# Layer norm of a two-layer decoder: order of sums, column products, mean spreads, root and first centering around the last tile

## The reference, cut to what matters

```python
def layer_norm(x, g, b):
    mu = jnp.mean(xf, axis=-1, keepdims=True)
    var = jnp.mean(jnp.square(xf - mu), axis=-1, keepdims=True)
    y = (xf - mu) * lax.rsqrt(var + LN_EPS)
    return (y * g + b)
...
for l in range(DEPTH):
    h = layer_norm(a * h + 0.5 * swiglu(h, ...), ln1_g[l], ln1_b[l])      # norms 1 and 4
    y = concat(pool_mixer(...), gla_mixer(...)) @ w_out[l]
    h = layer_norm(a * h + y, ln2_g[l], ln2_b[l])                         # norms 2 and 5
    h = layer_norm(a * h + 0.5 * swiglu(h, ...), ln3_g[l], ln3_b[l])      # norms 3 and 6
```

## Time and profile before

| | |
|---|---|
| median of 3 runs | 1818.94 us (1815.22 to 1819.45) |
| the profiled execution | 1817.18 us, its span 1815.5 us |
| PE busy | 1789.5 us, 99% of the span |
| DVE, ACT, POOL busy | 1424.3, 1164.0, 327.3 us |
| mean granted clock of TensorE | 0.99 of full speed |
| chain of work that ended last | PE 93%, DVE 4%, ACT 2% |
| column means on DVE (L1761) of norms 1 to 6 start at | 355.38, 556.59, 909.98, 1262.23, 1459.38, 1802.71 us |

### The profile page before, as it was taken

One profiled execution on the slowest core, in us unless ns is written; L12 is line 12 of the kernel. 1 busy time (PEld: TensorE's weight loads), 2 busy tenths in 40 slices (PEclk: granted clock), 3 DMA queues, 4 the chain that ended last, 5 costly groups with the idle time before them and its releaser, 6 DMA issues.

```text
span 1815.5 us, 37552 instructions
## 1 busy us (share of the span) xinstructions
PE 1789.5 (99%) x14440; PEld 1743.4 (96%) x14440; DVE 1424.3 (78%) x2545; ACT 1164.0 (64%) x2030; POOL 327.3 (18%) x366
## 2 busy tenths in 40 slices
PE   8999999999999999999999999999999999999997
PEld 8999999999999999999999999999998879999996
DVE  6988888668557988888688888886684589888886
ACT  5777676574347667676576676765743477777764
POOL 2111212211000121212301111122110111212113
PEclk9999999999999999999999999999999999999998
DMA  6675767556554676767556757565665656767662
GB/s 194 152 181 131 179 134 159 130 134 131 116 125 102 167 176 136 170 143 159 140 126 146 182 129 180 130 165 125 137 135 121 129 110 162 181 137 185 132 167 70
DMA packets 114081, 263.54 MB, mean 145 GB/s; under 512 B 10736, under 2 KB 37872, under 8 KB 113904
## 3 DMA queue, kind: packets, MB, share of 16 engines
q1 hardware_dynamic: 68112, 167.86, 31.9%
q0 software_dynamic: 45504, 92.29, 30.4%
q10 hardware_dynamic: 288, 0.98, 0.2%
HBM read 259.00 MB, written 2.10 MB: 144 GB/s over the span
## 4 chain that ended last, share of the span: by engine, by line
PE 93%; DVE 4%; ACT 2%; issue 1%; DMA 0%; ACTq 0%; SPq 0%; DVEq 0%
PE PS L629 21%; PE PS L630 21%; PE PS L631 21%; PE PS L608 4%; PE PS L609 3%; PE PS L610 3%; PE PS L563 3%; PE PS L565 3%; PE PS L564 3%; PE PS L599 2%; PE PS L573 2%; PE PS L574 2%; PE PS L927 1%; PE PS L770 1%; PE PS L758 1%
## 5 line engine op out<-in xcount | busy, mean ns | idle before, releaser
L503 POOL DMA_DIRECT2D w_lo<-in_stream x316 | 270.0, 854 | 1403.1 <-ACT w_lo L1138 1368.2
L1134 ACT ACTIVATE s_hi<-s_sum 128x512 fp32r<-128x512 f32 (+1 forms) x496 | 291.2, 588 | 153.2 <-PE PS L631 144.4
L1588 DVE TENSOR_TENSOR s_lo<-s_sum,s_hi 128x512 fp32r<-128x512 f32 (+1 forms) x496 | 293.5, 632 | 2.9 <-ACT s_hi L1134 2.7
L629 PE MATMUL PS<-v_hi,s_hi 128*128 128x264 f32 (+1 forms) x912 | 258.5, 283 | 0.0
L631 PE MATMUL PS<-v_hi,s_lo 128*128 128x264 f32 (+1 forms) x912 | 257.8, 283 | 0.0
L630 PE MATMUL PS<-v_lo,s_hi 128*128 128x264 f32 (+1 forms) x912 | 257.7, 283 | 0.0
L631 PE MATMUL PS<-x_hi,w_lo 128*128 128x264 f32 (+1 forms) x656 | 185.6, 283 | 0.0
L629 PE MATMUL PS<-x_hi,w_hi 128*128 128x264 f32 (+1 forms) x656 | 185.5, 283 | 0.0
L630 PE MATMUL PS<-x_lo,w_hi 128*128 128x264 f32 (+1 forms) x656 | 185.4, 283 | 0.0
L630 PEld LDWEIGHTS PS<-v_lo,s_hi 128*128 128x128 f32 x912 | 172.1, 189 | 0.0
L629 PEld LDWEIGHTS PS<-v_hi,s_hi 128*128 128x128 f32 x912 | 171.6, 188 | 0.0
(11 more groups left out here) (272 smaller groups left out, 5700.9 us busy)
## 6 DMA issues: line engine op xcount, KB each, us to landing
raw<-in_stream SPq DMA_DIRECT2D x164, 512.0 KB, 4.3
w_lo<-in_stream POOLq DMA_DIRECT2D x160, 256.0 KB, 4.6
spare<-in_stream SPq DMA_DIRECT2D x72, 512.0 KB, 6.5
w_lo<-in_stream POOLq DMA_DIRECT2D x60, 512.0 KB, 7.5
raw<-in_stream SPq DMA_DIRECT2D x48, 384.0 KB, 4.6
spare<-in_stream SPq DMA_DIRECT2D x48, 384.0 KB, 5.3
w_lo<-in_stream POOLq DMA_DIRECT2D x96, 192.0 KB, 4.7
X<-in_x_t SPq DMA_DIRECT2D x8, 264.0 KB, 6.7
```

What stands on the lines that cost most here:

```text
L503: pool.dma_start(w_lo[:, slot, to], stream[n // RAWS, n % RAWS, :, part], accum_op=ALU.add).then_inc(lo_added[slot], 16)
L629: nc.tensor.matmul(o, hi[:, w], r_hi, start=start and k == 0, stop=False, skip_group_check=True)
L1134: nc.scalar.activation(s_hi[:, j - 1, w], s_sum[:, j - 1, w], ACT.Copy).then_inc(S["s_hi_done"], 1)
L1588: V.tensor_tensor(s_lo[:, j - 1, w], s_sum[:, j - 1, w], s_hi[:, j - 1, w].bitcast(F32), ALU.subtract).then_inc(S["s_lo_done"], 1)
```

## The change

It touches nothing but order and waits around the end of `resid` and the beginning of `norm`, in all six norms.

- PE: M1 goes from behind Q1 to behind Q2. The order becomes C1, Q1, C2, Q2, M1, M2, R.
- DVE, sums: the square of tile 6 is added behind `add_last(0)`; `add_last(1)` stands ahead of `last_sum(0)`.
- DVE, norm: the reciprocal stands ahead of `center_first(0)`. In norms 1 to 5 tile 0 is centered straight from PSUM, as the last norm did already, so it waits for PE's spread and no longer for ACT's copy; tile 1 waits for the copy.
- ACT: the root stands ahead of the first copy of the mean. In norms 1 to 5 each copy waits until DVE has centered that half of tile 0 from the same PSUM half.

```diff
--- before.py
+++ after.py
@@ -780,12 +780,12 @@
                 columns(0, sum_x, 0)
                 pe.wait_ge(S["s2_first"], LN + 1)
                 columns(1, sum_sq, 0)
-                spread_mean(0).then_inc(S["mean_first"], 1)
 
                 pe.wait_ge(S["s1_done"], LN * 7 + 7)
                 columns(0, sum_x, 1).then_inc(S["mean_acc"], 1)
                 pe.wait_ge(S["s2_done"], LN * 7 + 7)
                 columns(1, sum_sq, 1).then_inc(S["msq_acc"], 1)
+                spread_mean(0).then_inc(S["mean_first"], 1)
                 pe.wait_ge(S["resid_done"], LN * KC + KC)
                 spread_mean(1).then_inc(S["mean_spread"], 1)
                 pe.wait_ge(S["rstd_done"], LN + 1)
@@ -1282,13 +1282,17 @@
                 def copy_mean(p):
                     return nc.scalar.activation(mean[:, tokens(span, p)], part(1, span, p), ACT.Copy)
 
-                act.wait_ge(S["mean_first"], LN + 1)
-                copy_mean(0).then_inc(S["mean_first_copied"], 1)
                 act.wait_ge(S["var_done"], LN + 1)
                 n_tok, blocks = stat_blocks(span)
                 nc.scalar.activation(col_std[0:n_tok, 0:blocks], col_var[0:n_tok, 0:blocks], ACT.Sqrt)\
                     .then_inc(S["std_done"], 1)
+                act.wait_ge(S["mean_first"], LN + 1)
+                if not final:
+                    act.wait_ge(S["centered_first"], LN + 1)
+                copy_mean(0).then_inc(S["mean_first_copied"], 1)
                 act.wait_ge(S["mean_spread"], LN + 1)
+                if not final:
+                    act.wait_ge(S["centered"], LN * KC + 1)
                 copy_mean(1).then_inc(S["mean_copied"], 1)
                 g = C_LN + 16 * r
 
@@ -1694,7 +1698,8 @@
                             dve.wait_ge(S["s1_done"], LN * 7 + (mo - 1))
                         V.tensor_tensor(sum_x[:, tok], X[:, 0, tok] if mo == 1 else sum_x[:, tok], X[:, mo, tok],
                                         ALU.add).then_inc(S["s1_done"], 1)
-                        add_square(mo)
+                        if mo < KC - 2:
+                            add_square(mo)
 
                 k = KC - 1
                 dve.wait_ge(S["s1_done"], LN * 7 + 6)
@@ -1721,8 +1726,9 @@
                         .then_inc(S["s2_done" if p else "s2_first"], 1)
 
                 add_last(0)
+                add_square(KC - 2)
+                add_last(1)
                 last_sum(0)
-                add_last(1)
                 last_square(0)
                 last_sum(1)
                 last_square(1)
@@ -1738,9 +1744,8 @@
                 def center_first(p):
 
                     h = tokens(span, p)
-                    if final:
-                        return V.tensor_tensor(X[:, 0, h], X[:, 0, h], part(1, span, p), ALU.subtract)
-                    return center(0, h)
+                    out = X[:, 0, h] if final else xhat[:, 0, h]
+                    return V.tensor_tensor(out, X[:, 0, h], part(1, span, p), ALU.subtract)
 
                 def center_spread(k):
 
@@ -1767,11 +1772,11 @@
                 V.scalar_tensor_tensor(out=col_var[0:n_tok, 0:blocks], in0=PS[0][0:n_tok, 1, 0:blocks], scalar=LN_EPS,
                                        in1=col_mean_sq[0:n_tok, 0:blocks], op0=ALU.add, op1=ALU.subtract)\
                     .then_inc(S["var_done"], 1)
-                dve.wait_ge(S["mean_first_copied"], LN + 1)
-                center_first(0).then_inc(S["centered_first"], 1)
                 dve.wait_ge(S["std_done"], LN + 1)
                 V.reciprocal(col_rstd[0:n_tok, 0:blocks], col_std[0:n_tok, 0:blocks]).then_inc(S["rstd_done"], 1)
-                dve.wait_ge(S["mean_copied"], LN + 1)
+                dve.wait_ge(S["mean_first_copied" if final else "mean_first"], LN + 1)
+                center_first(0).then_inc(S["centered_first"], 1)
+                dve.wait_ge(S["mean_copied" if final else "mean_spread"], LN + 1)
                 center_first(1).then_inc(S["centered"], 1)
                 if final:
                     for k in range(1, DVE_CENTERS):
@@ -1796,6 +1801,7 @@
                     V.tensor_tensor(x_lo[:, k, tok], X[:, k, tok], x_hi[:, k, tok].bitcast(F32),
                                     ALU.subtract).then_inc(S["x_lo_done"], 1)
 
+                dve.wait_ge(S["mean_copied"], LN + 1)
                 center(1).then_inc(S["centered"], 1)
                 for k in range(1, KC):
                     dve.wait_ge(S["centered"], LN * KC + (k + 1))
```

## The result

The changed kernel runs in 1820.83 us (median of 20 runs, 1815.54 to 1823.62); the kernel before ran in 1817.2 us beside it (median of 20, 1813.61 to 1820.40). The ratio is 1.0021 with a 95% interval of 1.0014 to 1.0027: slower by 3.8 us, between 2.5 and 4.9. The forecast of 1820.9 us stands 0.1 us from the measured median, and that closeness is luck. It was built on the first three runs of the kernel before, whose median of 1818.94 us lies 1.7 us above the median of 20, and its sum for the change, +2.0 us, is 1.8 us too small; the two errors cancel.

What follows compares the result with a forecast made beforehand. PE, busy 99%, was taken as the bound, so only its waits in the norms count. Terms 0.64 + 0.34 + 0.14 + 0.14 + 0.12 + 0.65 gave +2.0 us on 1818.94: 1820.9 us, range 1815.5 to 1823.8.

Steps and rivals of the forecast that it cites:

- The DVE order: DVE sums: first half's sum falls behind the second half's residual, which PE holds; C1 starts 0.67 us later, about 908.37.
- The two together: Later C1 against M1's 0.53 us and a 0.20 us wait saved on PE: variance taken as unmoved, within 0.05 us.
- The root: ACT: root ahead of the copies; it already started 0.04 us behind the variance's end, so effect taken as 0.
- M1 and M2 ahead of R: PE: two spreads delay R by 0.64 us in norm 1, 0.34 in norm 2, 0.12 to 0.14 in norms 3 to 5.
- the sign that I gave: In the changed profile, R starts directly behind M2 on PE, with no idle time and no wait for the reciprocal.
- Rival 3: Clock falls in every norm, ahead of M1, and both spreads run slow: 6.3 us slower, 1825.2 us; chance 0.06.
- The last norm: M2 comes later on PE at the lower clock, so the second half's centering starts 0.65 us late; 0.3 at full clock.
- Centering from PSUM: DVE centers from PSUM instead of SBUF: source makes no difference, 411 to 421 ns against at least 412; price 0.
- Rival 2: The clock falls less often, with no fall in norms 1, 2 and 4: 1816.3 us; chance 0.15.

Runs made afterwards that it cites:

- sums_only: The kernel before with only DVE's new order of sums; 1824.25 us, ratio 1.0042.
- old_sums: The changed kernel with the order of sums of the kernel before; 1815.28 us, ratio 0.9995.
- norm_only: The changed kernel without its new order of sums and with M1 back behind Q1; 1818.99 us, ratio 1.0016.
- norm_root: norm_only with a one-column root of a constant added on ACT ahead of the variance's root; 1817.49 us, ratio 1.0000.
- old_sums_root: old_sums with a one-column root of a constant added on ACT ahead of the variance's root; 1814.36 us, ratio 0.9983.
- after_root: The changed kernel with a one-column root of a constant added on ACT ahead of the variance's root; 1821.93 us, ratio 1.0027.
- after_fill: The changed kernel with four matmuls of constants on PE between the last product and C1; 1818.36 us, ratio 1.0003.
- sum_first: The changed kernel with the first half's sum moved ahead of tile 6's square on DVE; 1817.45 us, ratio 1.0005.

## Why the prediction was right, and where it was short

**The DVE order**: right, to the hundredth on DVE. The second half's residual is held by PE, the additions follow at 0.35 us and the first half's sum starts 0.35 us behind it. C1 came at 0.96 us, where I had 0.87 (908.37 - 907.50): it starts 0.14 us behind the sum's end (908.39 against 907.82 + 0.43), not 0.05. The 0.05 was Q1's distance; C1's own was in the rows, 907.70 against 907.12 + 0.43 = 907.55, that is 0.15.

**The two together**: right in kind, +0.06 us at the variance (3.08 against 3.02) where the clock has not fallen by then; I had taken 0 and bounded it by 0.05. The difference is C1's distance, taken from the wrong row. In norms 3 and 4 it is 0.70 and 0.81, and that is the clock, see below. sums_only shows the loss alone and old_sums the gain alone: what M1's place gives, the later sums take.

**The root**: I priced its move at nothing. It starts 0.09 us behind the variance instead of 0.04. That is 0.06 us at R where only M2 stands between Q2 and R (norm_only against norm_root), and nothing, or 0.03, behind M1 and M2 (old_sums against old_sums_root, norm 6 of after_root). Ahead of it ACT now waits 2.3 to 3.2 us, and the copy that stood there is gone; which of the two makes the 0.05 us was not separated.

**M1 and M2 ahead of R**: the number was right at full clock, 0.12 measured in norm 2 against a term of 0.14 at full clock and 0.34 with that norm's earlier fall. That it is so near is partly luck: two spreads in a row take 0.98 us, not 1.06, and the columns come 0.06 us later. M2 and the reciprocal end together, so R waits for both equally, and the sign that I gave, R behind M2 without a wait for the reciprocal, can't be read off this kernel. old_sums_root decides it: with the reciprocal 0.05 us earlier R stays, so that M2 alone holds it, as the prediction had it. In norm 2's term the fall at 557.48 was put in the middle of M2; with M2 from 557.41 on it lies at its start, and the same reckoning gives about 0.4 instead of 0.34.

**The step that was mis-sized** is the one at the lower clock. The prediction let the fall come where it came in the trace of before, at 3.0 us or later, and added 0.64 and 0.34 for norms 1 and 2. The place of the fall changes from norm to norm and from kernel to kernel; it came at 1.98 to 4.29 us in these two profiles. With the changed order everything from C1 to R is PE's and on the path: 1.67 and 1.78 us later at R than before for falls at 2.09 and 1.98, and 0.9 for one at 2.83. The kernel before had a pause of 0.4 us ahead of R, and only M2 behind Q2. Rival 3 named this mechanism, for all norms and with a chance of 0.06. In the changed kernel's profiled execution, the slowest of its 20, the clock did fall in all six norms (in four of them before), and two of the falls came ahead of M1; the profile of after_root has five such norms, that of after_fill one. The time at the lower clock, by contrast, has not grown over the runs (41 us against 40), so the change does not bring more of it, it pays more for it. The split of the 3.8 us stays an estimate: six norms of 0.12 to 0.30 give 0.9 us, and the rest, 2.9 us, would be two or three norms per execution with an early fall. The table above agrees with that, 3.3 us against 0.2, but it has three profiled executions for each order, and those of the changed kernel and of after_root are the slowest of theirs.

**The last norm**: 0.65 forecast. From the last product to the end 0.30 us were lost, because the clock fell only at 4.20, behind M2. That is the 0.3 given for full clock.

**Centering from PSUM**: the source makes no difference, as the trace had said. Half a tile of 264 tokens takes mostly 0.42 to 0.43 us from either. The Trainium skill (VectorE: DVE Perf Modes, the section on the TRN2 errata) gives a PSUM source 120 cycles of fixed cost and an SBUF source 58, by the prediction's estimate from that page 65 ns more; the trace does not agree with it. The twelve centerings of the changed kernel, by line:

```profile
L1748 DVE TENSOR_TENSOR xhat<-X,PS x10: 382/429/430, 356.6 to 1465.8; 128x264 f32<-128x264 f32 x8, 128x256 f32<-128x256 f32 x2
L1748 DVE TENSOR_TENSOR X<-X,PS x2: 421/422/422, 1810.3 to 1810.7; 128x256 f32<-128x256 f32 x2
```

**Rival 2** did not come: the time at the lower clock is what it was. **Open** stays why norm_only and norm_root differ by 0.0016 when their rows differ by 0.3 us. The intervals (1.0007 to 1.0024, 0.9991 to 1.0008) overlap at their ends, by the fit the two lie 1.4 us apart, give or take 0.9, and after_root shows no such gain. Open is also after_fill: by the fit it is at +3.2 us, while its profile shows 0.9 us at full clock and one early fall of 0.9.

## What to carry to other kernels

Before an operation is moved out of a chain, ask which operand the chain's first link waits for: here 0.53 us left PE's chain and the reordered sums held its start back by as much and a little more. Price small work ahead of a critical point at both clocks of TensorE and at every place where the clock may fall, since a pause in PE's queue is also a cushion; the useful filler (M1 between C1 and Q1) goes where PE waits anyway. Where a kernel's own runs spread by 0.3%, list each run's clock beside its time before a difference of 0.1% is explained.

## What the runs showed that I had not expected

- Instructions of one engine start at two distances behind their releaser. On ACT it is 0.03 to 0.04 us for the root before and for x_hi, and 0.09 to 0.10 for the root with the change and for the copies, these even after only 0.2 to 1.1 us of waiting; a root of a constant 0.3 us ahead brings the root back to 0.04. On PE it is 0.05 to 0.06 us for Q1 and R and 0.14 to 0.15 for C1, as long after 0.20 us of waiting (before) as after 0.96 (changed). What decides it was not found.
- Four matmuls of constants (eight in the trace) in 1 us of silence brought the time at the lower clock from 41 to 27 us per execution (after_fill), two such matmuls behind R brought it from 35 to 26 and from 38 to 28 us. Closing the silence ahead of C1 by starting C1 earlier did not (sum_first, 41 us).
- Each of the two matmuls that the trace counts for a mean spread of 264 columns of 32-bit values takes 0.245 us at 2.4 GHz (0.98 for four) and about 0.475 at 1.2 GHz (1268.26 - 1266.36 = 1.90 for four).
